# ScalarE's Gelu ahead of the square roots, and VectorE's convolution ahead of the output tables, in the channel rounds of a decoder layer

## What is computed

```python
def token_mixer(h, ...):
    z = einsum('bld,de->ble', h, w_in)
    x_lru, g_lru, u_s5, gate_a, gate_b = split(z, SPLITS)
    y_a = gelu(g_lru) * rg_lru(causal_depthwise_conv(x_lru, conv_w, conv_b), wa, ba, wx, bx, lam)
    y_s = gelu(s5_ssm(u_s5, ...))
    ...                                   # gates, GLU, output projections, MoE

def rg_lru(x, wa, ba, wx, bx, lam):       # 1536 channels, 16 heads of 96
    r = sigmoid(x @ wa + ba); i = sigmoid(x @ wx + bx)        # per head
    log_a = -8 * r * softplus(-lam); a = exp(log_a)
    mult = sqrt(-expm1(2 * log_a)); mult[first token] = 1
    return scan(h = a * h + mult * i * x)

def s5_ssm(u, ...):                       # 64 groups of 16 channels, 64 complex states each
    # diagonal complex recurrence per group, y = Re(C h) + d * u
```

## Time and profile before

| | us |
|---|---|
| median of three runs | 1550.81 (1544.0 to 1551.45) |
| the profiled execution | 1536.16 |
| its span, first to last instruction | 1534.4 |
| TensorE matmul busy | 1415.3 (92%) |
| VectorE busy | 868.9 (57%) |
| ScalarE busy | 606.2 (40%) |
| GpSimd busy | 466.3 (30%) |

### The profile page before, as it was taken

One profiled execution on the slowest core, in us unless ns is written; L12 is line 12 of the kernel. 1 busy time (PEld: TensorE's weight loads), 2 busy tenths in 40 slices (PEclk: granted clock), 3 DMA queues, 4 the chain that ended last, 5 costly groups with the idle time before them and its releaser, 6 DMA issues.

```text
span 1534.4 us, 18525 instructions
## 1 busy us (share of the span) xinstructions
PE 1415.3 (92%) x6293; PEld 936.8 (61%) x6293; DVE 868.9 (57%) x1240; ACT 606.2 (40%) x847; POOL 466.3 (30%) x415
## 2 busy tenths in 40 slices
PE   6979898979799999999996799999999999999990
PEld 4456666667588888645442566666666666666660
DVE  4598758583910001045632577667776666666755
ACT  3114444545722222101011455555555555555540
POOL 1012424243544444200073133332222322333322
PEclk8999898989899999999997899999999999999995
DMA  8034242524233333670045599999999999999953
GB/s 242 1 110 78 61 80 60 81 58 63 76 90 109 93 100 89 236 301 15 0 165 180 222 354 359 364 363 361 361 363 360 361 360 371 363 365 362 361 176 123
DMA packets 141491, 315.97 MB, mean 206 GB/s; under 512 B 18898, under 2 KB 100514, under 8 KB 116160
## 3 DMA queue, kind: packets, MB, share of 16 engines
q1 hardware_dynamic: 125984, 281.50, 53.0%
q0 software_dynamic: 15456, 33.79, 9.3%
HBM read 297.35 MB, written 34.65 MB: 216 GB/s over the span
## 4 chain that ended last, share of the span: by engine, by line
DMA 38%; PE 37%; issue 9%; DVE 6%; POOL 5%; ACT 2%; POOLq 2%; DVEq 1%; SPq 0%; ACTq 0%
DMA acc_dram<-arena 36%; PE bank L701 8%; PE bank L702 8%; PE bank L703 8%; PE bank L919 4%; PE bank L735 3%; DVE arena L1335 2%; POOL slot_dram L623 2%; PE bank L933 2%; PE bank L708 2%; POOL arena L648 1%; ACT arena L1116 1%; POOLq L589 1%; PE bank L834 1%; POOL arena L590 1%
## 5 line engine op out<-in xcount | busy, mean ns | idle before, releaser
L1335 DVE TENSOR_TENSOR gate_up_low<-gate_up,gate_up_high 128x1024 fp32r<-128x1024 f32 x256 | 296.4, 1219 | 94.0 <-ACT gate_up_high L1116 94.0
L1116 ACT ACTIVATE arena<-bank 96x512 f32<-96x512 f32 (+5 forms) x248 | 131.3, 553 | 410.6 <-PE bank L1059 140.2
L1116 ACT ACTIVATE gate_up_high<-gate_up 128x1024 fp32r<-128x1024 f32 x256 | 249.5, 1047 | 54.7 <-DMA gate_up<-moe_w_up_in 40.2
L1059 PE MATMUL bank<-down,arena 128*96 128x512 f32 x512 | 230.4, 592 | 1.0 <-DVE arena L1848 1.0
L1335 DVE TENSOR_TENSOR arena<-arena 128x512 f32<-128x512 f32 (+10 forms) x286 | 197.5, 722 | 44.5 <-POOLq L579 26.0
L701 PE MATMUL bank<-gate_up_high,rows_high 128*96 128x512 f32 x512 | 207.8, 406 | 5.1 <-DVE rows_low L1335 5.0
L703 PE MATMUL bank<-gate_up_high,rows_low 128*96 128x512 f32 x512 | 204.2, 399 | 0.0
L702 PE MATMUL bank<-gate_up_low,rows_high 128*96 128x512 f32 x512 | 202.7, 396 | 0.0
L708 PEld LDWEIGHTS bank<-arena 96*128 96x128 f32 (+4 forms) x1001 | 129.5, 191 | 100.7 <-issue 47.2
L708 PE MATMUL bank<-arena 96*128 96x96 f32 (+4 forms) x1001 | 129.9, 271 | 52.2 <-ACT arena L1116 29.4
L554 POOL TENSOR_TENSOR wb_low<-arena,wb_high 128x1024 fp32r<-128x1024 f32 (+1 forms) x40 | 105.7, 2643 | 150.9 <-ACT wb_high L1116 150.9
(11 more groups left out here) (150 smaller groups left out, 2176.1 us busy)
## 6 DMA issues: line engine op xcount, KB each, us to landing
gate_up<-moe_w_gate_in SPq DMA_DIRECT2D x64, 1024.0 KB, 11.8
gate_up<-moe_w_up_in SPq DMA_DIRECT2D x64, 1024.0 KB, 18.8
down<-moe_w_down_in SPq DMA_DIRECT2D x64, 1024.0 KB, 12.9
arena<-w_in_in SPq DMA_DIRECT2D x40, 512.0 KB, 4.1
arena<-w_glu_in SPq DMA_DIRECT2D x16, 512.0 KB, 4.0
arena<-w_lru_out_in SPq DMA_DIRECT2D x8, 768.0 KB, 4.9
arena<-x_in SPq DMA_DIRECT2D x8, 512.0 KB, 5.0
arena<-w_in_in SPq DMA_DIRECT2D x2, 2048.0 KB, 12.1
```

Of the source, the lines that this page charges most:

```text
L1059: last = mm(banks[5 + hf][0:SL, :], heT[u % 2][:, k], dn[u % 4][:, k, hs], start=(k == 0), stop=(k == 1))
L1116: return nc.scalar.activation(out_, in_, func, **kw)
L1335: return V_.tensor_tensor(out_, a, b_, op)
```

## The change

In ScalarE's program the four Gelus of Y (with their wait for k_stored) go ahead of the three square roots, and from the second round on high_a(0) of the g weights goes ahead of the first Identity instead of the third. In VectorE's program tables_out of rounds 1 to 3 goes from the end of the round before to behind the convolution of its own round.

```diff
@@ ScalarE
             for b in range(NB):
                 for m in range(ML):
-                    if m == 2:
+                    if m == (2 if b == 0 else 0):
                         high_a(0, 2 * b + 1)
                     ch = ML * b + m
                     act.wait_ge(S["xproj_put"], ML * b + m + 1)
@@ ScalarE, behind Exp and Tanh
-                for m in range(ML):
-                    act.wait_ge(S["mult2_ready"], ML * b + m + 1)
-                    f(rr[:, m, :], rr[:, m, :], ACT.Sqrt).then_inc(S["mult_ready"], 1)
                 act.wait_ge(S["k_stored"], 16 * (b + 1))
                 for n in range(4):
...
                       ACT.Gelu_apprx_tanh).then_inc(S["Y_kept"], 1)
+                for m in range(ML):
+                    act.wait_ge(S["mult2_ready"], ML * b + m + 1)
+                    f(rr[:, m, :], rr[:, m, :], ACT.Sqrt).then_inc(S["mult_ready"], 1)
@@ VectorE, behind the convolution
                     ins.then_inc(S["conv_done"], 1)
+                if b:
+                    tables_out(b)
                 decays(b)
@@ VectorE, behind the recurrence
-                if b + 1 < NB:
-                    tables_out(b + 1)
```

## The result

The changed kernel takes 1571.3 us (median of four runs, 1567.77 to 1574.71), the kernel before beside it 1549.81 (four runs): a ratio of 1.0151, 95% interval 1.0124 to 1.0178, or 21.5 us more. Forecast were 1576.6, range 1558 to 1586. The profiled execution took 1567.77 us with a span of 1566.0.

The account below looks back on a forecast made before the run. TensorE's own queue and a 7.4 us hole were taken to bound each round; K's delay 5.4 plus clock 3.2 makes 8.6 us at three boundaries, 25.8 on 1550.8: 1576.6 us, range 1558 to 1586.

Parts of the forecast that it names:

- turns done, wait for wa_low at x_proj(1): On TensorE after the earlier turns: a wait of 2 us for GpSimd's first wa_low stays at x_proj(1).
- TensorE and ScalarE ready for K: Ahead of the K products: both engines ready at 263.4 instead of 272.2, 8.8 us earlier.
- the tables' length: VectorE's tables behind the convolution: 8.1 us undisturbed, lengthened by GpSimd's two wa_low (2.1, 2.4) and dI product (0.6).
- K later than before: K products on TensorE wait for Q_ready, at 277.6 instead of 272.2: +5.4 us, bounds +3.5 to +6.9.
- the clock's cost: TensorE's 1.2 GHz stretch moves behind K's start after 14 us idle: 3.2 us, bounds 1.7 to 3.6.
- the tail: Round 3's end: VectorE's eight s_low still wait for the last lru_done; 0, within 1.5 us either way.
- The chain: At each round boundary K waits for VectorE's recurrence, convolution and tables, delayed by GpSimd's collisions; K +5.4 us.
- Both undecided signs in part 2 and 3: On VectorE beside GpSimd: scans block (lru_done 3.8 us later, 2.5 if not); the memset costs nothing (bound 1.5).
- (a): Rival at the boundaries: collisions cost VectorE nothing, the clock costs 3.2 us; 0 per round, 1550 us; chance 0.07.
- (b): Rival: collisions cost nothing and the clock holds over a 5.3 us wait; 10 us less, 1541 us; chance 0.04.
- (c): Rival: K does not wait for the tables; each boundary gains 7 to 9 us, 1525 us; chance 0.04.
- (d): Rival: K held but the clock not lost; 16 us more, 1567 us; chance 0.85 together with the forecast.

Follow-up runs that it names:

- the held splits: The changed kernel with GpSimd's splits of the second and third g weights held until Q_ready: 1558.73 us beside 1547.31 for the kernel before, ratio 1.0072.
- one more product: The changed kernel with one more split-sized GpSimd product between its two splits in rounds 1 to 3: 1561.32 us beside 1536.35 for the kernel before.
- the run with one repetition: The changed kernel with g_proj(1)'s products run once more ahead of K, results unused: 1551.62 us beside 1536.35 for the kernel before, ratio 1.0107.

## Why the prediction was right, and where its terms were off

Counted in us behind the first mult2 (234.00 before, 239.83 changed), the steps stand like this:

| step | forecast | measured |
|---|---|---|
| turns done, wait for wa_low at x_proj(1) | 2 us | 1.7 us, three times |
| TensorE and ScalarE ready for K | 29.4 | 28.9 |
| GpSimd's first g split starts | 12.9 | 13.9 |
| lru_done | 22.5 | 22.5 |
| convolution ends | 30.4 | 30.7 |
| the tables' length | 13.2 | 12.1 |
| K starts | 43.6 | 42.8 |
| K later than before | +5.4 | +4.65 |
| the clock's cost | +3.2 | +1.9 |
| per boundary | 8.6 | 6.6 |
| three boundaries | 25.8 | 20.1 |
| the tail | 0, within 1.5 | not told from the spread |

**The chain.** That K waits for one engine's queue, recurrence, convolution, tables, was right in every link, and so was the place of each collision: the first split and the U2 copy in the recurrence, the next two splits on the tables. The run with ScalarE's edits alone removes the whole loss, the held splits remove 4 us a boundary of it, one more product adds 2.4.

**The tables.** 12.1 us instead of 13.2. One by one, the two tensor_tensors that met the two splits took 2.87 and 3.49 us and the one that met the dI product 1.62, where the form takes 1.36: 1.5, 2.1 and 0.3 us, where I had taken 2.1, 2.4 and 0.6. The memset of 275.48 to 277.06 blocked nothing: the split before it ends at 275.5, the blocked tensor_tensor is over at 276.75 and the next takes its plain 1.36. The scan did block (3.38 us at 253.80). Both undecided signs in part 2 and 3 came out as the sum had them. By the Trainium skill (SBUF — State Buffer, "SBUF: two separate sides") just that was to be expected: two SBUF inputs take the shared ports against a GpSimd operation that reads SBUF; now rows show both cases.

**The clock.** This is the term that was mis-sized most. I took the cost of the slow stretch from the turns of before, 7.15 us long. Behind K's start it lasts some 3.9 us only, and costs 1.92 us. The bounds, 1.7 to 3.6, held it. What was wrong in this term is the carrying of a slow stretch's length from one place to another. Why it is 3.9 us here stays open: other runs have other lengths behind the same wait (last section).

**What held the forecast.** It had 25.8 us and 21.5 were measured. Both terms of the boundary came out smaller than forecast, K's delay by 0.75 us and the clock by 1.3, so the forecast is not right by one error cancelling another. The chain was right, and the range was wide enough for the sizes.

**The rivals.** (a) and (b) fall with the blocked instructions. (c), that the hole at the turns would go and nothing come in its place, is nearly what ScalarE's edits alone do: 20 us gained where it said 25. (d) is the run with one repetition, in part: with K at full clock the period is 80.45 instead of 81.88.

What I had not seen is how much hung on the one line of high_a(0). I priced it at 3.8 us on the recurrence; putting it back takes 28 us off (21.5 over the kernel before becomes 6.4 under it), because the split goes beside the convolution, its followers fall behind the tables instead of on them (4 us), the opening and the convolution come 3.6 us earlier, and TensorE, itself later by the wait for the split, uses the time.

## What to carry to other kernels

Two moves that are each harmless (+0.1% and -1.3%) can cost 1.5% together: an engine that becomes early exposes whatever was put behind its old arrival time, so price a move against the schedule that the other edits make, not against the profile in hand. Before moving work on VectorE, list which of its instructions take all their inputs from SBUF and when GpSimd will run: here the convolution's steps, which read PSUM and SBUF, were the ones that could stand beside GpSimd's work. And when two profiles differ by more than their medians, find a mark behind the changed stage before explaining the difference.

## What the runs showed of the hardware that was not expected

The length of the 1.2 GHz stretch behind an idle TensorE is not one number, and the wait in front of it does not give it. Behind 7.4 us of idling it was about 7.1 us, behind 14.7 us 3.9 us. Even the same wait gives different lengths within one run. These are K products of the run with one more product of GpSimd:

```profile
204.09 5.13 PE L838 MATMUL bank<-arena 64*16 64x128 f32 x64 [16.84 <-DVEq L1336]
...
372.24 6.36 PE L838 MATMUL bank<-arena 64*16 64x128 f32 x64 [16.84 <-DVEq L1336]
```

Short waits behave the same way: behind 2.19 us K took 5.34 and 3.67 us in the run with VectorE's move alone, and with ScalarE's edits alone it took 3.67 us behind 2.48 and 5.12 us behind 2.50. So a wait of some 2.2 us at K can already cost 1.7 us more, and may cost nothing; what decides it is not shown.

VectorE and GpSimd alternate where GpSimd reads SBUF and VectorE takes all its inputs from there. In the changed kernel two splits of 2.4 us and the first two tensor_tensors of the tables pass each other one by one, and a blocked instruction's waiting is counted in its length (3.38 for 1.23 us). A one-input copy of GpSimd blocks a two-input product of VectorE as well (2.17 for 0.69 us beside the copy of 256.05). And a one-input copy of VectorE is blocked too: in the run with the splits held, the copy behind the tables takes 2.62 us beside a split that starts with it, against 0.43 us at 282.70 in the changed kernel.

```profile
276.28 2.62 DVE L1543 COPY arena<-arena 128x512 f32<-128x512 f32 x1
```

The routing stage with its small indirect stores and gathers took 201.8 to 202.8 us in five profiles and 213.1 to 214.5 in the other eight, with the same code, 0.7% of the whole. The profiles taken on one chip agree, but whether a chip keeps to one of the two is not shown: on one of them two runs of the same kernel took 9 us more than two others (the run with one repetition), and only one of these was profiled.
